# Where the first norm's squares, sums and ones products are made, in a two-block transformer kernel

## The reference

```python
def rms_norm(x, gain):
    y = x32 * lax.rsqrt(jnp.mean(x32 * x32, axis=-1, keepdims=True) + EPS)
    return (y * gain.astype(jnp.float32)).astype(x.dtype)

def swiglu_ffn(h, w_in, w_out):
    gate, up = jnp.split(h @ w_in, 2, axis=-1)
    return (jax.nn.silu(gate) * up) @ w_out

# first statement of layer 0:
h = h + 0.5 * swiglu_ffn(rms_norm(h, ffn_norm[0, 0]), ffn_w_in[0, 0], ffn_w_out[0, 0])
```

## Time and profile before

| | us |
|---|---|
| median of 3 runs | 3986.89 |
| lowest, highest run | 3974.49, 3989.94 |
| profiled execution | 3988.59 |
| its span, first to last instruction | 3986.8 |
| TensorE busy | 3386.2 (85%) |
| VectorE busy | 1673.8 (42%) |
| ScalarE busy | 692.8 (17%) |

### The profile page before, as it was taken

The page is one execution under the profiler, slowest core; times in us unless marked ns, Lnnn a source line. Parts: engine busy times, 40 slices in busy tenths (PEclk is TensorE's granted clock), DMA queues, the critical chain, the costliest instruction groups (busy, mean ns, idle before and its releaser), DMA issues. The chain is left out here.

```text
span 3986.8 us, 47764 instructions
## 1 busy us (share of the span) xinstructions
PE 3386.2 (85%) x16698; PEld 2380.5 (60%) x16698; DVE 1673.8 (42%) x4095; ACT 692.8 (17%) x1483; POOL 596.4 (15%) x516
## 2 busy tenths in 40 slices
PE   8998779999895878989977888887699777888876
PEld 7875558878673767877866333433378663334433
DVE  2113541111226542111243767677412437676774
ACT  1101211011002211100131212222101312122221
POOL 0000000000000000000000544444100005444441
PEclk9999779999997998999989889999899898889998
DMA  4342014434240003423323999999433239999994
GB/s 166 147 152 93 2 50 140 150 134 155 108 150 0 1 0 107 175 110 142 134 95 144 422 421 421 421 421 421 195 139 138 86 142 422 421 422 421 421 421 193
DMA packets 113622, 827.68 MB, mean 208 GB/s; under 512 B 12528, under 2 KB 14064, under 8 KB 15120
## 3 DMA queue, kind: packets, MB, share of 16 engines
q0 software_dynamic: 73728, 536.90, 32.4%
q1 hardware_dynamic: 37184, 273.59, 18.8%
q10 hardware_dynamic: 2576, 15.59, 1.1%
HBM read 824.99 MB, written 1.05 MB: 207 GB/s over the span
## 5 line engine op out<-in xcount | busy, mean ns | idle before, releaser
L2144 PE MATMUL psum_all<-expert_rows,const_sb 128*128 128x512 f32 x2048 | 998.4, 646 | 260.9 <-ACT const_sb L2090 260.0
L1935 POOL DMA_INDIRECT expert_rows<-in_peer_uv_dram,head_experts x512 | 596.2, 1164 | 3322.1 <-issue 2272.1
L2144 PEld LDWEIGHTS psum_all<-expert_rows,const_sb 128*128 128x128 f32 x2048 | 413.7, 207 | 828.4 <-issue 490.9
L2025 DVE CUSTOM_DVE_ANT_0 expert_rows<-expert_rows,xn 128x1024 f32<-128x1024 f32 x512 | 618.0, 1223 | 318.5 <-DMA expert_rows<-in_peer_uv_dram,head_experts 312.9
L261 PE MATMUL psum_all<-xn,weight_ring 128*128 128x272 f32 (+1 forms) x3200 | 732.0, 392 | 0.0
L261 PEld LDWEIGHTS psum_all<-xn,weight_ring 128*128 128x128 f32 x3200 | 613.3, 192 | 118.6
L261 PE MATMUL psum_all<-hidden,weight_ring 128*128 128x272 f32 (+1 forms) x1408 | 318.6, 389 | 0.0
L261 PEld LDWEIGHTS psum_all<-hidden,weight_ring 128*128 128x128 f32 x1408 | 267.5, 190 | 50.5
L1653 PE MATMUL psum_all<-x,weight_ring 128*128 128x256 f32 x1024 | 229.8, 383 | 0.0
L2090 ACT ACTIVATE const_sb<-cst,head_weights 128x128 f32<-128x128 f32 x512 | 163.6, 390 | 323.8 <-DVE head_weights L2031 318.2
L1653 PEld LDWEIGHTS psum_all<-x,weight_ring 128*128 128x128 f32 x1024 | 193.5, 191 | 29.0 <-issue 3.1
(11 more groups left out here) (473 smaller groups left out, 3049.4 us busy)
## 6 DMA issues: line engine op xcount, KB each, us to landing
weight_ring<-in_ffn_in_dram SPq DMA_DIRECT2D x88, 1024.0 KB, 4.8
weight_ring<-in_w_in_dram SPq DMA_DIRECT2D x48, 1024.0 KB, 5.5
weight_ring<-in_ffn_out_dram SPq DMA_DIRECT2D x32, 1408.0 KB
weight_ring<-in_peer_q_dram SPq DMA_DIRECT2D x16, 1024.0 KB
weight_ring<-in_hyb_in_dram SPq DMA_DIRECT2D x12, 1024.0 KB, 4.8
wv<-in_w_v_dram ACTq DMA_DIRECT2D x8, 1024.0 KB, 7.2
weight_ring<-in_br_attn_dram SPq DMA_DIRECT2D x8, 1024.0 KB, 5.8
weight_ring<-in_br_lru_dram SPq DMA_DIRECT2D x8, 1024.0 KB
```

The source lines that it names most:

```text
L1935: pool.indirect_dma_start(out=rows[:, j, :], out_offset=None, in_=a["peer_uv"], in_offset=bass.IndirectOffsetOnAxis(ap=idx[:, n, j:j + 1], ...
L2025: dve.tensor_tensor_reduce(row, row, xt[:, n, :], 1.0, 0.0, ALU.mult, ALU.add, dots[:, n, j:j + 1]).then_inc(S.dotted, 1)
L2144: mm = pe.matmul(sums(n, half), diag[:, j, :], rows[:, j, D + half * 512:D + (half + 1) * 512], start=False, stop=last and j == TOPK - 1)
```

## The change

The eight squares and six sums of the first norm leave the first phase and are issued at the start of the first feed-forward phase, on ScalarE and VectorE, with semaphores of their own (`first_squares`, `first_summed`). The two ones products go behind the first weight tile on TensorE: `gemm_pe` gets an argument `early`, a function that is called after slot 0 of the first pair. For that the first pair of this product is written out ahead of the loop, and the loop starts at 1. In the first feed-forward TensorE waits for the sums and squares before the ones products. The first phase loses the semaphores `squares` and `summed` and gains a wait of VectorE for its own eight scalings. All four feed-forward phases lose the unused semaphore `consts` and gain the two new ones.

```diff
-def gemm_pe(pe, w, region, count, halves, rhs, banks, ready, free, ktiles=KD, hidden=None):
-    with pe.Fori(0, count // 2) as i:
+def gemm_pe(pe, w, region, count, halves, rhs, banks, ready, free, ktiles=KD, hidden=None, early=None):
+    def pair(i):
         for s in range(2):
...
                 mm.then_inc(ready, 1)
+            if early is not None and s == 0 and isinstance(i, int):
+                early()
+
+    if early is not None:
+        pair(0)
+    with pe.Fori(0 if early is None else 1, count // 2) as i:
+        pair(i)
...
                 @block.tensor
                 def _(pe):
-                    norm_pe(pe, S, ones, norm, banks[7], cols)
-                    gemm_pe(pe, w, g % 2, KF, 2, xn[:, :, cols], banks[0:4], S.tile_ready, S.bank_free)
+                    def sums():
+                        if g == 0:
+                            pe.wait_ge(S.first_summed, KD - 2)
+                            pe.wait_ge(S.first_squares, KD)
+                        norm_pe(pe, S, ones, norm, banks[7], cols)
+
+                    if g:
+                        sums()
+                    gemm_pe(pe, w, g % 2, KF, 2, xn[:, :, cols], banks[0:4], S.tile_ready, S.bank_free, early=None if g else sums)
...
                 @block.scalar
                 def _(act):
+                    if g == 0:
+                        for m in range(KD):
+                            square_tile(act, S._replace(summed=S.first_summed), x, norm, m, S.first_squares, cols)
                     norm_act(act, S, rs, banks[7])
...
                     dve.sem_inc(S.hidden_ready, 2)
+                    if g == 0:
+                        for m in range(2, KD):
+                            sum_tile(dve, S._replace(summed=S.first_summed), norm, m - 1, S.first_squares, cols)
                     norm_dve(dve, S, step, rs)
...
-            with phase(nc, "x_in", "vec_in", "ones_in", *NEXT_NORM) as (block, S):
+            with phase(nc, "x_in", "vec_in", "ones_in", "scaled") as (block, S):
...
                     act.dma_start(vcs, a["vec"]).then_inc(S.vec_in, 16)
-                    act.wait_ge(S.x_in, 16 * 2)
-                    for m in range(KD):
-                        square_tile(act, S, x, norm, m, S.squares, whole)
                     act.wait_ge(S.vec_in, 16)
...
                         dve.tensor_scalar(xn[:, m, :], x[:, m, :], gain[:, m:m + 1], None, ALU.mult).then_inc(S.scaled, 1)
-                        if m >= 2:
-                            sum_tile(dve, S, norm, m - 1, S.squares, whole)
+                    dve.wait_ge(S.scaled, KD)
```

More of the change, by code:

```diff
@@ L303, in ffn @@
             rs = norm.rs[:, cols]
-            with phase(nc, *NORM, *NEXT_NORM, "tile_ready", "bank_free", "gate_ready", "hidden_ready", "out_ready", "out_free", "consts",
+            with phase(nc, *NORM, *NEXT_NORM, "tile_ready", "bank_free", "gate_ready", "hidden_ready", "out_ready", "out_free", "first_squares", "first_summed",
                        shared=w.landed[(g + 1) % 2]) as (block, S):
```

## The result

The changed kernel takes 4006.62 us (median of six runs, 4002.43 to 4011.45) against 3987.93 us (median of six, 3974.49 to 3989.94): a ratio of 1.0054, 95% interval 1.0039 to 1.0069. It is 18.7 us slower, where 3.9 us less was forecast, and it lies outside the range.

The account below looks back on a forecast made before the run. TensorE was taken to bound the kernel from 13.91 us to the first feed-forward's end. Starting it earlier (13.88 - 9.66), less 0.22 and 0.1, gives 3.9 us: 3986.9 - 3.9 = 3983.0 us, range 3969 to 3993.

Parts of the forecast that it names:

- TensorE's start: End of first phase: without sums between them the scalings end sooner, so TensorE starts at 9.66 us against 13.88.
- rival B: Start of the first product: the first weight tile lands late and holds TensorE, gain only 1.9 us, 3985.0; chance 0.05.
- The squares and sums: Second phase, beside TensorE's first tile: table load, then a chain of 6.49 us, done at 17.4 us, slack 1.7 us.
- Rival A: TensorE's new wait ahead of the ones products: sums come late, TensorE idles; at half pace 3.1 us slower, 3990.0; chance 0.06.
- The slow start: TensorE's first instructions run slowly; passed once in either order, so reordering costs nothing and the first tile takes 9.72 us.
- The four ones products: Behind the first weight tile on TensorE: four instructions at 0.229 us, 0.92 us in all, from 19.1 to 20.0.
- rs: Result of the root and reciprocal behind the ones products, ready at 22.6 us; TensorE's third tile has 4.4 us of slack.
- The clears: Semaphore clears: each of four feed-forward phases has one more, 4 x 0.06 = 0.22 us later in all.
- The sum, 3.9 us: Whole program: earlier TensorE start (13.88 - 9.66), less 0.22 for clears and 0.1 for waits and loop entry.
- The written-out pair adds 128 instructions ... to TensorE's list and no work: First input product: 64 products and 64 weight loads more in the list; two waits and loop entry put at 0.1 us.
- rival C: TensorE's later loops: moved code is fetched anew each round, at most 4.4 us a round; 16 to 23 us slower; chance 0.03.
- D: Later phases: the edit works but something later gives the gain back, time 3986.9 us; no place known; chance 0.06.

Follow-up runs that it names:

- slots 0: Changed kernel with TensorE's chunk loop laid on the first instruction of a fetched block of 256; 3980.24 us, ratio 0.9993 to the kernel before.
- 42: Kernel before with its chunk loop laid on instruction 42 of a fetched block; one execution, 3977.47 us beside 3990.23 for the kernel before.
- 56: Kernel before with its chunk loop laid on instruction 56 of a fetched block; one execution, 3983.92 us beside 3990.23 for the kernel before.
- 160: Kernel before with its chunk loop laid on instruction 160 of a fetched block; one execution, 4000.68 us beside 3990.23 for the kernel before.
- slot 104: Kernel before with its chunk loop laid on instruction 104 of a fetched block; one execution, 3988.45 us beside 3990.23 for the kernel before.
- shift by 64: Kernel before with 62 semaphore increments in TensorE's first phase, moving all its later code by 64 instructions; 3990.08 us, ratio 1.0020 to the kernel before.

## Why the prediction was wrong

The part about the change was right to within 0.6 us in the first two phases, and of the signs that the prediction named only the last square fell outside (17.75 us, where 16 to 17.5 was named). All of them lie in the first 262 us, and none could tell of the phase at 1279 us where the time was lost.

- TensorE's start: 9.66 us forecast, 10.23 measured. The scalings followed each other at 0.27 us as read (eight in 2.26 us); x landed 0.24 us later in this execution, the barrier took 0.17 us more than forecast and let ScalarE go at 10.08, and TensorE started 0.15 us behind it. The row puts that start down to the first weight tile, but the tile had landed at 9.4 us (issued at 2.2, 7.2 on its way), so rival B did not come.
- The squares and sums: table load right behind the barrier, chain of 6.38 us, done at 17.75 (17.4 forecast), 1.6 us ahead of TensorE's weight load for the ones products at 19.40. Rival A did not come. The table load ended at 11.36 and the next activation started at 11.37. The Trainium skill's page "ScalarE: Activation LUTs", section "What ACT_TABLE_LOAD costs", puts a drain of 1.38 us there; this trace shows none.
- The slow start was passed once, as said: the first tile took 9.4 us of TensorE. The four ones products ran at the steady pace from 19.63 (19.1 forecast; the next tile's began 0.91 us later), rs was done at 23.0 (22.6), no gap opened at the third tile, and the second tile's L342 stood at 28.19 (27.6).
- The clears: 0.06 us more at each feed-forward, as counted.
- The sum, 3.9 us, measured 3.8 at the end of the first phase and 3.1 ahead of the chunk loop.

The step that failed is "The written-out pair adds 128 instructions ... to TensorE's list and no work", with rival C at 0.03. C was the right mechanism at the wrong loops and price. I asked which loops return most often and took the product loops, 9 and 3 returns, at up to 4.4 us each; and I held against it that five input loops at five places show no idle time. Those input loops are 135 instructions long, the output loops 182. They were no evidence for a loop of 1750, whose body I did not count: 424 products of four instructions each (two weight loads and two products for one float32 product) and 54 others. Its four returns cost 29.0 us in the phase, 7.2 each. The wait that I had priced at up to 4.4 us was about that long (3.4 to 4.3), but VectorE kept TensorE waiting for 1.7 us at each return before, so only 2.3 of it are new. The sum had no term for the rest: 3.7 us a return in which TensorE does the same products at the lower clock (0.92 against 0.98 over the phase, 417 ns a product instead of 269 where it is low), and 1.3 in other waits of the round.

The Trainium skill's page "Runtime: NRT & Kernel Launch", section "Instruction fetch mechanics", which the prediction cited for C, also gives the size that I did not use: TensorE's instruction memory holds 2048 instructions, refilled by blocks of 256, which is eight blocks. The runs agree in part: a loop of 6.84 blocks stays at hand at slots 0, 42 and 56 and does not at 160. But the loop touches eight blocks at 56, 104 and 160 alike, so the size alone doesn't tell these apart. The same section also speaks of a window of two blocks; by that every return of this loop would fetch, and the kernel before (7 packets in the whole phase) shows otherwise. That the block behind the loop, fetched ahead, is what pushes the first one out fits with nine packets a return for a body of eight, but was not shown apart.

The other rivals: D had no place and none was found. The chance of slower by over 0.5% stood at 0.03, and the measured change is just at that bound; the range, built from the spread of the runs, left no room for C.

What stays open: why with slot 104 and with the shift by 64 two of the four returns fetch (the second and third in the one, the second and fourth in the other), and what makes the clock fall inside a round.

## What to carry to other kernels

Before code is added to an engine's list, count the body of every loop behind it in instructions, whatever the loop computes, and compare the longest with what that engine holds; the instruction queue's packets per phase show in one row whether a loop is fetched anew. Price a fetch by more than its wait: here the longer waits at the returns cost 9.1 us, and the lower clock 14.6. A loop close to that size should be pinned (a start at a chosen place, or a hint for its return), or else each edit ahead of it draws a lot worth up to 29 us here, seven times the edit's own gain. And when an edit ahead of everything changes the time, take the difference phase by phase before explaining it.

## What was not expected of the hardware

- A loop of 1750 TensorE instructions either stays at hand, or is fetched whole (nine packets of 16 KB a return), or, in between, at two of its four returns; the cost was 7.2 us a return in the changed kernel and 4.8 in the shift by 64.
- With an idle time of 3.4 to 4.3 us at a return the granted clock fell to 0.50 each time in the changed kernel; with one of 1.7 us, four times in the kernel before, it did not.
- One hint instruction at the head of the loop took the packets from 96 to 60 with the code at its bad place.
- A semaphore increment on TensorE took about 0.16 us: with 125 of them at the head of the chunk phase its first product came 20.0 us into the phase.
